# One load for the constants, the first query chunk ahead of the modulation chunks, and its products woven between the modulation pairs

## The chip, the cores and the metric

The kernel runs on one core of one Trainium2 chip. The time is the device time of one execution in microseconds (us); smaller is better. TensorE is PE in the profile (PEld its weight loads), VectorE is DVE, ScalarE is ACT, GpSimd is POOL and SyncE is SP.

## The reference

One layer of a diffusion backbone over 640 tokens (128 of context, 512 of latent) with 1024 channels, in float32. Cut to the part that the change touches:

```python
mod = silu(c) @ w_mod + b_mod                 # 6 x 1024 values, for context and latent each
shift1, scale1, gate1, shift2, scale2, gate2 = split(mod, 6)
h = rmsnorm(x, g_norm1) * (1 + scale1) + shift1
proj = h @ w_in + b_in                        # q, k, v, o, 32 gate columns, pooling, branch gates
y_a, C, n, m = mlstm_branch(q, k, v, o, gates, ...)      # two scans over time, eight heads
y_b = pool_branch(u_pool, ...)
x = x + gate1 * ((sigmoid(g_a) * (y_a @ w_a) + sigmoid(g_b) * (y_b @ w_b)) @ w_out)
x = x + gate2 * hier_moe(rmsnorm(x, g_norm2) * (1 + scale2) + shift2)   # 16 experts
```

No column of `proj` can be finished before all 1024 channels of `h` are there, and `h` needs the first third of `mod` (shift1 and scale1).

## The kernel before

Channels lie on the partitions. `xT`, `hn`, `hhi` and `hlo` each have eight blocks k of 128 channels x 640 tokens. Float32 products are made of three passes: each factor is split into a part `hi` that TensorE takes in its fast float32 form and a rest `lo`, and `three` adds hi*hi, hi*lo and lo*hi. ScalarE makes the hi part by a copy (`split_hi`, L573), VectorE the lo part by a subtraction (`split_lo`, L912).

Weights come in chunks of 1 MB (128 x 2048), in the order of one list (`wst`), through four buffers `raw[0]` to `raw[3]`. SyncE issues them in order (L373) and waits before each until its buffer is free: chunk c needs that chunk c-4 has been used. A chunk of the projection is free after its `split_lo`, a chunk of `w_mod` after the matmuls that read it. The list begins with the eight chunks of `w_mod` for shift1 and scale1, then come eight groups of one query or key chunk and two chunks of the rest of `w_mod`, then four value chunks.

The program up to the value stage:

- ScalarE issues eight loads of constants (L588: `cin`, `cst`, `col`, `wgr`, `bg`, `m0`, `wr`, `br`), all on one semaphore, and waits for all of them. SyncE issues the four loads of `xT`, then the chunks.
- Norm: ScalarE squares the eight blocks of `xT` (L594), GpSimd adds them (L435), TensorE sums over the partitions with a matrix of ones, ScalarE makes `rstd` (L580 and L581), VectorE multiplies (L935).
- First third of `mod`, in four rounds i: TensorE multiplies `csil` by two chunks (`mod_half`, L1489; two of them are a pair here), ScalarE copies the row out of PSUM (L601), TensorE turns it into columns (`mod_columns`), VectorE adds the bias and makes `gain` (L949, L952), then scales and shifts blocks 2i and 2i+1 of `hn` (L957); ScalarE makes `hhi` (L606) and VectorE `hlo` (L942). Round i+1 of TensorE starts behind round i.
- When all four rounds are through, TensorE takes the first query chunk block by block (L1521 on): for each k the 32 gate columns and the chunk's two blocks of 128 columns, 18 matmuls of 320 tokens, each time behind `hlo` of that k. The gates then go through ScalarE and VectorE (L609 to L971).
- j = 1 to 7: `block_q(j, 0)`, `mod_columns` of the group before, `mod_half`, `block_q(j, 1)`, `mod_half` (L1551 on). The `mod_half` calls of j = 0 stand right behind the first query chunk. Then the value stage (L1600 on), four chunks by five token tiles.

## Time and profile before

| what | value |
|---|---|
| median of three runs | 1082.78 us (1082.72 to 1090.57) |
| the profiled execution | 1087.06 us, span 1084.8 us |
| PE busy | 969.8 us (89%) |
| DVE, ACT, POOL busy | 599.0, 486.2, 139.2 us |
| mean granted TensorE clock | 0.951 |
| moved by DMA | 216.36 MB, 199 GB/s over the span |

The span is the time from the first to the last instruction of the profiled execution; its own time is the span and 2.3 us around it. In the page's 40 slices (27.1 us each) PE is at 0, 5, 8 and 8 tenths in the first four and at 9 in nearly all that follow; slice 30 has 2 and 8 around it, and the last two have 6 and 0.

### The profile page before, as it was taken

What the parts mean: (1) busy time and instruction counts of PE and PEld (TensorE: products, weight loads), DVE (VectorE), ACT (ScalarE), POOL (GpSimd) and SP (SyncE); (2) the same over time, 40 slices, a digit from 0 to 9 for tenths busy, and PEclk for the clock granted to TensorE, in tenths of its full rate; (3) what the DMA queues carried; (4) which work ended last, traced back from release to release, by engine and by line L of the source; (5) the groups of instructions that cost most, each with busy time, mean ns of one, the idle gap of its engine ahead of it and who ended that gap; (6) DMA issues with size and microseconds to landing.
All of it is one profiled execution on the core that took longest, in us unless ns stands there. A gap on an engine that the chain in (4) does not pass through costs nothing.

```text
span 1084.8 us, 13868 instructions
## 1 busy us (share of the span) xinstructions
PE 969.8 (89%) x5654; PEld 853.8 (79%) x5654; DVE 599.0 (55%) x751; ACT 486.2 (45%) x640; POOL 139.2 (13%) x135
## 2 busy tenths in 40 slices
PE   0588999999999999999999999982899999999960
PEld 0266888888788989999998998882788888888850
DVE  0432330123476758222115445536599999999986
ACT  2213222223557575222224123223578787888853
POOL 1200000000101000796000000001012111111120
PEclk9868999999999999999999999985899999999995
DMA  7453454551324223232221124522899999999945
GB/s 285 169 199 117 161 206 182 191 184 39 88 83 126 81 66 123 111 131 84 79 78 45 73 78 167 242 85 71 350 379 406 423 420 421 411 420 416 391 190 208
DMA packets 36063, 216.36 MB, mean 199 GB/s; under 512 B 4352, under 2 KB 4800, under 8 KB 15520
## 3 DMA queue, kind: packets, MB, share of 16 engines
q1 hardware_dynamic: 26064, 179.32, 42.4%
q0 software_dynamic: 8112, 32.53, 8.6%
q10 hardware_dynamic: 1824, 3.64, 0.9%
q8 instruction: 44, 0.72, 0.3%
q14 instruction: 19, 0.16, 0.1%
HBM read 200.68 MB, written 14.79 MB: 199 GB/s over the span
## 4 chain that ended last, share of the span: by engine, by line
PE 86%; DVE 6%; DMA 3%; ACT 3%; issue 1%; POOL 1%; ACTq 0%; DVEq 0%; POOLq 0%
PE ps L1449 81%; PE ps L1489 2%; DMA br<-in_br 1%; PE ps L1829 1%; POOL hn L435 1%; DMA yscr<-yb,slot_rows 1%; PE ps L1847 1%; DVE xr L1427 1%; DVE rowB L1424 1%; DVE hn L935 1%; DMA xg<-h2scr,slot_rows 1%; DVE xr L1431 0%; PE ps L1780 0%; PE ps L1712 0%; DVE OFF L1075 0%
## 5 line engine op out<-in xcount | busy, mean ns | idle before, releaser
L1449 PE MATMUL ps<-hhi,whi 128*128 128x320 f32 x672 | 156.7, 315 | 5.1 <-DVE wlo L917 5.1
L917 DVE TENSOR_TENSOR wlo<-raw,whi 128x2048 fp32r<-128x2048 f32 x29 | 68.0, 2348 | 167.8 <-ACT whi L576 167.8
L1449 PE MATMUL ps<-hlo,whi 128*128 128x320 f32 x672 | 154.5, 311 | 0.0
L1449 PE MATMUL ps<-hhi,wlo 128*128 128x320 f32 x672 | 154.5, 311 | 0.0
L1449 PEld LDWEIGHTS ps<-hhi,whi 128*128 128x128 f32 x672 | 113.1, 190 | 17.2 <-DVE wlo L917 6.0
L1449 PEld LDWEIGHTS ps<-hhi,wlo 128*128 128x128 f32 x672 | 113.7, 190 | 0.0
L1449 PEld LDWEIGHTS ps<-hlo,whi 128*128 128x128 f32 x672 | 113.5, 190 | 0.0
L576 ACT ACTIVATE whi<-raw 128x2048 fp32r<-128x2048 f32 x29 | 55.3, 1909 | 96.8 <-PE ps L1449 68.6
L1324 DVE TENSOR_TENSOR wlo<-raw,whi 128x2048 fp32r<-128x2048 f32 x32 | 72.6, 2288 | 5.2 <-ACT whi L844 5.2
L1324 DVE TENSOR_TENSOR olo<-raw,ohi 128x2048 fp32r<-128x2048 f32 x32 | 72.4, 2286 | 4.5 <-ACT ohi L844 4.5
L844 ACT ACTIVATE whi<-raw 128x2048 fp32r<-128x2048 f32 x32 | 61.3, 1919 | 18.3 <-PE ps L1449 18.3
L844 ACT ACTIVATE ohi<-raw 128x2048 fp32r<-128x2048 f32 x32 | 61.3, 1919 | 17.8 <-PE ps L1449 17.8
L534 POOL DMA_INDIRECT xg<-h2scr,slot_rows x16 | 18.6, 1160 | 360.3 <-DVE slot_rows L1377 246.5
L1449 PE MATMUL ps<-hhi,owh 128*128 128x320 f32 x160 | 58.2, 380 | 0.0
L1449 PE MATMUL ps<-whi,xgh 128*128 128x512 f32 x128 | 51.3, 401 | 2.4 <-DVE xgl L1331 2.4
L771 ACT ACTIVATE TH<-ps,col 128x640 f32<-128x640 f32 x16 | 12.7, 796 | 88.6 <-PE ps L1449 88.6
L1449 PE MATMUL ps<-ohi,xgh 128*128 128x512 f32 x128 | 50.6, 396 | 0.0
L1449 PE MATMUL ps<-whi,xgl 128*128 128x512 f32 x128 | 50.5, 394 | 0.0
L1449 PE MATMUL ps<-wlo,xgh 128*128 128x512 f32 x128 | 50.4, 393 | 0.0
L1449 PE MATMUL ps<-ohi,xgl 128*128 128x512 f32 x128 | 50.0, 391 | 0.0
L1449 PE MATMUL ps<-olo,xgh 128*128 128x512 f32 x128 | 49.9, 390 | 0.0
L544 POOL DMA_INDIRECT yscr<-yb,slot_rows x16 | 31.3, 1953 | 138.1 <-ACT yb L864 130.4
(314 smaller groups left out, 2095.9 us busy)
## 6 DMA issues: line engine op xcount, KB each, us to landing
raw<-in_wexp SPq DMA_DIRECT2D x64, 1024.0 KB, 9.0
raw<-in_wst SPq DMA_DIRECT2D x60, 1024.0 KB, 4.9
eraw<-in_wexp SPq DMA_DIRECT2D x32, 1024.0 KB, 8.3
nm<-negscr POOLq DMA_DIRECT2D x8, 640.0 KB, 7.1
wib<-wiscr POOLq DMA_DIRECT2D x8, 512.0 KB, 6.2
xT<-in_x SPq DMA_DIRECT2D x4, 640.0 KB, 7.1
xr<-in_xt SPq DMA_DIRECT2D x1, 2560.0 KB, 9.1
h2scr<-ht ACTq DMA_DIRECT2D x5, 512.0 KB, 3.6
```

Source lines behind the costliest of these rows:

```text
L435: gp.tensor_tensor(sq[:, 0, :], sq[:, 0, :], sq[:, k, :], ALU.add)\
L534: gp.indirect_dma_start(xg[p % 2][:, :], None, h2scr, bass.IndirectOffsetOnAxis(ap=slot_rows[:, 0, e:e + 1], axis=0)).then_inc(d_xg[p % 2] ...
L544: gp.indirect_dma_start(yscr, bass.IndirectOffsetOnAxis(ap=slot_rows[:, 1, e:e + 1], axis=0), yb[p % 2][:, :], None).then_inc(d_sc, 16)
L576: act.activation(dst[:, :], raw[raw_slot(c)][:, :], ACT.Copy).then_inc(hi_ready, 1)
L771: act.activation(halves(TH[:, gate_at(f), :]), pair(E_TH[f]), ACT.Tanh, scale=0.5, bias=col[:, 36 + f:37 + f]).then_inc(pair_free[E_TH[f] ...
L844: act.activation(ehi[i % ESPL][:, :], eraw[s][:, :], ACT.Copy).then_inc(e_hi, 1)
L917: dve.tensor_tensor(lo[:, :], raw[s][:, :], f32(hi[:, :]), ALU.subtract)\
L935: st.on(dve.tensor_tensor(hn[:, k, :], xT[:, k, :], rstd[:, :], ALU.mult))
L1324: dve.tensor_tensor(elo[i % ESPL][:, :], eraw[s][:, :], f32(ehi[i % ESPL][:, :]), ALU.subtract).then_inc(e_free[s], 1)
L1424: dve.scalar_tensor_tensor(rowB[:, t, :], rowB[:, t, :], wab[:, 1, t:t + 1], gate2[:, c, :], ALU.mult, ALU.mult).then_inc(f_y, 1)
L1449: return nc.tensor.matmul(out, lhsT, rhs, start=start, stop=stop)
L1489: last = nc.tensor.matmul(ps[32 * kk:32 * kk + 32, bank, :], csil[:, 4 * kh + kk, :], raw[slot][:, kk * 512:(kk + 1) * 512], start=kh == 0 ...
```

## The change

The constants become one tensor `small` (128 x 1440) with one load on SyncE's queue, ahead of `xT`; `wgr` has a load of its own behind `xT`. The first query chunk is the first of the list, ahead of the eight chunks of `w_mod`; the last group of `w_mod` stands right ahead of the values. VectorE adds the squares in place of GpSimd. ScalarE scales and shifts the blocks in place of VectorE (L609 of the new program). TensorE weaves the eight block steps of the first query chunk (`keys_outer`) between the pairs, and each group of the rest of `w_mod` is taken one j later, the last one in the value stage. The diff, cut to its core:

```diff
-AT_QK = N_MOD1
-AT_V = AT_QK + N_QK + N_MOD2
+AT_M1, AT_QK = 1, N_MOD1 + 1
+AT_V = N_MOD1 + N_QK + N_MOD2
...
+
+
+def m2_at(g):
+    return AT_QK + 1 + 3 * g if g < N_QK - 1 else AT_V - 2
...
 
         @block.sync
         def _(sp):
+            sp.dma_start(small[:, :], small_d).then_inc(d_const, 16)
             for k in range(0, KT, 2):
                 sp.dma_start(xT[:, k:k + 2, :], x_d[:, k:k + 2, :]).then_inc(d_x[k // 2], 16)
+            sp.dma_start(wgr[:, :, :], wg_d).then_inc(d_wg, 16)
             for s in range(NRAW):
                 sp.sem_inc(raw_free[s], 1)
...
             gp.memset(gOne[:, :], 1.0).then_inc(s_init, 1)
 
-            def sum_squares(sq, done, n=KT):
-
-                gp.wait_ge(done[0], 1)
-                for k in range(1, n):
-                    gp.wait_ge(done[0], k + 1)
-                    if k > 1:
-                        gp.wait_ge(done[1], k - 1)
-                    gp.tensor_tensor(sq[:, 0, :], sq[:, 0, :], sq[:, k, :], ALU.add)\
-                      .then_inc(done[1], 1)
-
-            sum_squares(hn, (s_sq, s_sum1))
...
-            smalls = [(cin[:, :, :], c_d), (cst[:, :], cst_d), (col[:, :], col_d),
-                      (wgr[:, :, :], wg_d), (bg[:, :], bg_d), (m0[:, :], m0_d),
-                      (wr[:, :, :], wr_d), (br[:, :], br_d)]
-            assert len(smalls) == N_SMALL
-            for dst, src in smalls:
-                act.dma_start(dst, src).then_inc(d_const, 16)
-            act.wait_ge(d_const, 16 * N_SMALL)
+            act.wait_ge(d_const, 16)
             act.activation(csil[:, :, 0:2], cin[:, :, :], ACT.Tanh, scale=0.5).then_inc(s_csil, 1)
             for k in range(KT):
                 if k % 2 == 0:
                     act.wait_ge(d_x[k // 2], 16)
                 act.activation(hn[:, k, :], xT[:, k, :], ACT.Square).then_inc(s_sq, 1)
+            act.wait_ge(d_wg, 16)
             act.activation(wgh[:, :, :], wgr[:, :, :], ACT.Copy).then_inc(s_wgh, 1)
             act.preload_act_table_set(LN_EXP)
+            split_hi(0, QH[0])
             act.wait_ge(s_ssq, 1)
             inv_rms(halves(rstd[:, :]), ps[:, 0:2, 0:HALF], D, s_rstd)
             for i in range(4):
-                chunk_used(act, 2 * i + 1)
-                act.activation(mrow1[:, i, :], ps[:, 2 + i, :], ACT.Copy).then_inc(s_mrow, 1)
-                if i == 3:
-                    split_hi(AT_QK, QH[0])
+                chunk_used(act, AT_M1 + 2 * i + 1)
+                if i >= 2:
+                    act.wait_ge(s_modT, i - 1)
+                act.activation(mrow1[:, i % 2, :], ps[:, 4, :], ACT.Copy).then_inc(s_mrow, 1)
+                act.wait_ge(s_gain, i + 1)
                 for k in (2 * i, 2 * i + 1):
-                    act.wait_ge(s_hn, k + 1)
+                    for c, a, b in ((0, 0, TC), (1, TC, T)):
+                        act.activation(hn[:, k, a:b], hn[:, k, a:b], ACT.Identity,
+                                       bias=mod[:, k, c:c + 1], scale=gain[:, k, c:c + 1])\
+                           .then_inc(s_hn, 1)
+                    act.wait_ge(s_hn, 2 * k + 2)
                     act.activation(hhi[:, k, :], hn[:, k, :], ACT.Copy).then_inc(s_hhi, 1)
+            split_hi(qk_at(1), QH[1])
 
             act.wait_ge(s_gps, 1)
...
-            for j in range(N_QK):
-                if j:
-                    act.wait_ge(q_used, j)
-                split_hi(AT_QK + 3 * j + 3, QH[(j + 1) % 2])
+            block_qk(0)
+            block_qk(1)
+            for j in range(1, N_QK):
+                act.wait_ge(q_used, j)
+                split_hi(qk_at(j + 1) if j < N_QK - 1 else AT_V, QH[(j + 1) % 2])
                 block_qk(2 * j)
                 block_qk(2 * j + 1)
-                mod_row2(j)
+                mod_row2(j - 1)
 
             act.wait_ge(q_used, N_QK)
             split_hi(AT_V + 1, QH[1])
+            mod_row2(N_QK - 1)
...
-                st.on(dve.tensor_tensor(hn[:, k, :], xT[:, k, :], rstd[:, :], ALU.mult))
+            for k in range(1, KT):
+                dve.wait_ge(s_sq, k + 1)
+                if k > 1:
+                    dve.wait_ge(s_sum1, k - 1)
+                dve.tensor_tensor(hn[:, 0, :], hn[:, 0, :], hn[:, k, :], ALU.add).then_inc(s_sum1, 1)
             dve.wait_ge(s_wgh, 1)
             dve.tensor_tensor(wgl[:, :, :], wgr[:, :, :], f32(wgh[:, :, :]), ALU.subtract)\
                .then_inc(s_wgl, 1)
+            split_lo(0, QH[0], QL[0])
+
+            def normalise(k):
+                st.on(dve.tensor_tensor(hn[:, k, :], xT[:, k, :], rstd[:, :], ALU.mult))
 
             def input_lo(k):
                 dve.wait_ge(s_hhi, k + 1)
                 dve.tensor_tensor(hlo[:, k, :], hn[:, k, :], f32(hhi[:, k, :]), ALU.subtract)\
                    .then_inc(s_hlo, 1)
 
+            dve.wait_ge(s_rstd, 1)
+            for k in range(4):
+                normalise(k)
             for i in range(4):
                 dve.wait_ge(s_modT, i + 1)
                 both = mod[:, 0:16, :].rearrange("p (s k) c -> p s k c", s=2)[:, :, 2 * i:2 * i + 2, :]
                 bias = col[:, B_MOD:B_MOD + 16].rearrange("p (s k) -> p s k", s=2)
-                st.do(dve.tensor_tensor(both, ps[:, 0, 448 + 8 * i:456 + 8 * i].rearrange(
+                st.do(dve.tensor_tensor(both, ps[:, 5, 0:8].rearrange(
                     "p (s k c) -> p s k c", s=2, c=2), by(bias[:, :, 2 * i:2 * i + 2].unsqueeze(3),
                                                           [P, 2, 2, 2]), ALU.add))
-                st.do(dve.scalar_tensor_tensor(
+                dve.scalar_tensor_tensor(
                     gain[:, 2 * i:2 * i + 2, :], mod[:, 8 + 2 * i:10 + 2 * i, :], 1.0,
-                    by(col[:, G_1 + 2 * i:G_1 + 2 * i + 2].unsqueeze(2), [P, 2, 2]), ALU.add, ALU.mult))
-                for k in (2 * i, 2 * i + 1):
-                    for c, a, b in ((0, 0, TC), (1, TC, T)):
-                        ins = dve.tensor_scalar(hn[:, k, a:b], hn[:, k, a:b], gain[:, k, c:c + 1],
-                                                mod[:, k, c:c + 1], ALU.mult, ALU.add)
-                    ins.then_inc(s_hn, 1)
-                if i == 3:
-                    split_lo(AT_QK, QH[0], QL[0])
+                    by(col[:, G_1 + 2 * i:G_1 + 2 * i + 2].unsqueeze(2), [P, 2, 2]), ALU.add, ALU.mult)\
+                   .then_inc(s_gain, 1)
+                if i < 2:
+                    normalise(4 + 2 * i)
+                    normalise(5 + 2 * i)
                 for k in (2 * i, 2 * i + 1):
                     input_lo(k)
+            split_lo(qk_at(1), QH[1], QL[1])
 
             dve.wait_ge(s_gate, 2)
...
+            def mod_pair(i):
+                if i:
+                    pe.wait_ge(s_mrow, i)
+                mod_half(AT_M1 + 2 * i, 0, 4)
+                mod_half(AT_M1 + 2 * i + 1, 1, 4)
+
+            def mod_turned(i):
+                if i:
+                    pe.wait_ge(s_gain, i)
+                pe.wait_ge(s_mrow, i + 1)
+                mod_columns(mrow1[:, i % 2, :], ps[:, 5, 0:8])
+
+            pe.wait_ge(d_const, 16)
+            square_sums(hn, s_sum1, s_ssq)
+            pe.wait_ge(s_csil, 3)
+            mod_pair(0)
+            mod_turned(0)
+            mod_pair(1)
+            pe.wait_ge(s_wgl, 1)
+            pe.wait_ge(s_rstd, 1)
+            chunk_split(0)
+            keys_outer(0)
+            mod_turned(1)
+            keys_outer(1)
+            mod_pair(2)
+            keys_outer(2)
+            mod_turned(2)
+            keys_outer(3)
+            mod_pair(3)
+            keys_outer(4)
+            mod_turned(3)
+            for k in (5, 6, 7):
+                keys_outer(k)
...
-            for j in range(N_QK):
-                if j:
-                    block_q(j, 0)
-                    pe.wait_ge(m_done, j - 1)
-                    pe.wait_ge(s_mrow, 4 + j)
-                    mod_columns(mrow, ps[:, 7, 0:8])
+            def mod2_turned(g):
+                pe.wait_ge(m_done, g)
+                pe.wait_ge(s_mrow, 5 + g)
+                mod_columns(mrow, ps[:, 7, 0:8])
+
+            for j in range(1, N_QK):
+                block_q(j, 0)
+                if j >= 2:
+                    mod2_turned(j - 2)
                 else:
                     pe.wait_ge(s_gate, 2)
-                mod_half(AT_QK + 3 * j + 1, 0, 6)
-                if j:
-                    block_q(j, 1)
+                mod_half(m2_at(j - 1), 0, 6)
+                block_q(j, 1)
                 pe.sem_inc(q_used, 1)
-                mod_half(AT_QK + 3 * j + 2, 1, 6)
+                mod_half(m2_at(j - 1) + 1, 1, 6)
...
                 for t in range(NT):
                     value_block(c, t)
                     if c == 0 and t == 0:
-                        pe.wait_ge(m_done, N_QK - 1)
-                        pe.wait_ge(s_mrow, 4 + N_QK)
-                        mod_columns(mrow, ps[:, 7, 0:8])
-                    if c == 0 and t == 3:
+                        mod2_turned(N_QK - 2)
+                        mod_half(m2_at(N_QK - 1), 0, 6)
+                        mod_half(m2_at(N_QK - 1) + 1, 1, 6)
+                    if c == 0 and t == 2:
+                        mod2_turned(N_QK - 1)
+                    if c == 0 and t == 4:
```

Three places in the programs. In the rows `raw_67` to `raw_70` are the four weight buffers of the program before and `raw_61` to `raw_64` those of the new one; `whi_71` and `whi_65` are the hi part of the first query chunk; `mrow` is a row of `mod`, and a matmul from it is a `mod_columns`. L1449 and L1489 before are L1466 and L1506 now.

TensorE at its start, before:

```order
L1449 MATMUL ps<-hn,cst 128x320 [waits s_sum1,s_csil,d_const]
...
L1489 MATMUL ps<-raw_67,csil 32x512 [waits raw_full0]
...
L1489 MATMUL ps<-raw_68,csil 32x512 [waits raw_full1]
...
L1449 MATMUL ps<-cst,mrow_83 128x2 [waits s_mrow,s_rstd]
...
L1489 MATMUL ps<-raw_69,csil 32x512 [waits raw_full2]
```

and now:

```order
L1466 MATMUL ps<-hn,small 128x320 [waits s_sum1,d_const]
...
L1506 MATMUL ps<-raw_62,csil 32x512 [waits raw_full1,s_csil]
...
L1506 MATMUL ps<-raw_63,csil 32x512 [waits raw_full2]
...
L1466 MATMUL ps<-small,mrow_77 128x2 [waits s_mrow]
...
L1506 MATMUL ps<-raw_64,csil 32x512 [waits raw_full3,s_mrow]
...
L1506 MATMUL ps<-raw_61,csil 32x512 [waits raw_full0]
...
L1466 MATMUL ps<-hhi,wgh 48x320 [waits raw_free0,s_hlo,s_rstd,s_wgl]
```

The first block step now stands behind the second pair; the second pair's last chunk uses the buffer of the first query chunk.

ScalarE in the first round, before and then now:

```order
L596 ACT_TABLE_LOAD
L580 ACTIVATE rstd<-ps,cst 128x640 [waits s_ssq]
L581 ACTIVATE rstd<-rstd 128x640 [waits act_steps]
L601 ACTIVATE mrow_83<-ps 128x512 [waits raw_free1]
L606 ACTIVATE hhi<-hn 128x640 [waits s_hn] x2
```

```order
L582 ACTIVATE whi_65<-raw_61 128x2048 [waits raw_full0]
L586 ACTIVATE rstd<-ps,small 128x640 [waits s_ssq]
L587 ACTIVATE rstd<-rstd 128x640 [waits act_steps]
L605 ACTIVATE mrow_77<-ps 128x512 [waits raw_free2]
L609 ACTIVATE hn<-hn,mod,gain 128x128 [waits s_gain]
L609 ACTIVATE hn<-hn,mod,gain 128x512
L613 ACTIVATE hhi<-hn 128x640 [waits s_hn]
```

The hi part of the first query chunk is made ahead of `rstd`, and two operations per block have come to ScalarE.

TensorE from the last chunk of the query stage into the value stage, before and then now (L1601 and L1643 turn the gathered values of `mod`):

```order
L1489 MATMUL ps<-raw_70,csil 32x512 [waits raw_full3]
...
L1449 MATMUL ps<-whi_71,hhi 128x512 [waits v_free,q_free,raw_free0]
...
L1449 MATMUL ps<-cst,mrow 128x2 [waits s_mrow,m_done]
...
L1449 MATMUL ps<-whi_71,hhi 128x512 [waits v_free,q_free]
...
L1601 MATMUL ps<-cst,mst 64x128 [waits s_mst]
```

```order
L1506 MATMUL ps<-raw_62,csil 32x512 [waits raw_full1]
...
L1466 MATMUL ps<-whi_65,hhi 128x512 [waits v_free,q_free,raw_free0]
...
L1466 MATMUL ps<-small,mrow 128x2 [waits s_mrow,m_done]
...
L1506 MATMUL ps<-raw_63,csil 32x512 [waits raw_full2]
...
L1506 MATMUL ps<-raw_64,csil 32x512 [waits raw_full3]
...
L1466 MATMUL ps<-small,mrow 128x2 [waits s_mrow,m_done]
...
L1643 MATMUL ps<-small,mst 64x128 [waits s_mst]
```

Two chunks of `w_mod` and a second turning have come into the first value chunk.

## Rows read from the trace of the kernel before

**Rows 1.** Busy time by window: window, length, engines, granted clock, DMA share, GB/s.

```profile
0.00:97.00 97.00, 47.20 (x261) 32.13 (x262) 27.23 (x52) 26.51 (x35) 11.66 (x13) 0.87 0.54 202
102.00:560.00 458.00, 456.27 (x3007) 416.28 (x3007) 186.21 (x383) 166.80 (x358) 76.78 (x89) 1.00 0.34 117
```

**Rows 2.** The chain of waits, 0 to 110 us: start, length, what.

```profile
4.81 16.04 DMA br<-in_br
...
22.49 1.54 POOL hn L435
...
34.22 2.49 PE ps L1449 x4
...
38.33 5.97 DVE hn L935 x8
...
53.40 0.61 ACT mrow L601
54.05 1.87 PE ps L1449 x8
...
66.33 21.75 PE ps L1449 x132
...
92.57 1.81 ACT whi L576
...
96.82 10.39 PE ps L1449 x56
```

**Rows 3.** DMA 0 to 22 us in 40 slices, total; landing of `xT`, of `raw`.

```profile
GB/s 0 0 0 112 168 214 410 382 425 424 413 401 449 430 390 429 409 417 404 448 404 380 473 410 358 462 415 381 421 428 384 445 391 376 453 420 403 417 283 30
DMA packets 2112, 7.73 MB, mean 351 GB/s; under 512 B 576, under 2 KB 960, under 8 KB 1600
DMA to landing us min/median/max: 4.4/7.1/9.6
DMA to landing us min/median/max: 4.8/6.7/17.4
```

**Rows 4.** Two modulation pairs in the timeline, then windows as in group 1.

```profile
36.62 3.64 PE L1489 MATMUL ps<-raw,csil 128*32 128x512 f32 x16
42.03 1.92 PE L1489 MATMUL ps<-raw,csil 128*32 128x512 f32 x16
...
44.00:47.90 3.90, 0.00 (x0) 0.00 (x0) 3.74 (x10) 1.94 (x3) 0.00 (x0) 0.93 0.99 376
48.00:62.00 14.00, 12.57 (x56) 6.42 (x56) 7.05 (x17) 5.89 (x7) 0.00 (x0) 0.50 0.88 327
66.30:70.80 4.50, 4.47 (x17) 4.15 (x18) 1.40 (x2) 0.00 (x0) 0.00 (x0) 0.50 0.69 240
71.10:88.00 16.90, 16.90 (x116) 15.87 (x115) 0.00 (x0) 0.00 (x0) 0.00 (x0) 1.00 0.00 1
```

**Rows 5.** Groups by form on ACT and DVE: busy us, mean ns, idle before.

```profile
L594 ACT ACTIVATE hn<-xT 128x640 f32<-128x640 f32 x8 | 5.1, 719 | 0.0
L672 ACT ACTIVATE DG<-nmd,a_tok 128x128 f32<-128x128 f32 x80 | 25.1, 398 | 11.1 <-PE ps L1449 9.8 <-DVE nmd L1054 1.3
L681 ACT ACTIVATE OFF<-nm,a_tok 128x384 f32<-128x384 f32 x16 | 9.9, 616 | 0.0
L942 DVE TENSOR_TENSOR hlo<-hn,hhi 128x640 fp32r<-128x640 f32 x8 | 6.2, 820 | 0.3
L917 DVE TENSOR_TENSOR wlo<-raw,whi 128x2048 fp32r<-128x2048 f32 x2 | 4.6, 2287 | 1.1 <-ACT whi L576 1.1
```

**Rows 6.** One j of the query stage: chain of waits, then ACT's timeline.

```profile
107.21 0.99 PE ps L1489 x8
108.21 7.24 PE ps L1449 x48
...
116.44 8.02 PE ps L1449 x56
...
121.48 1.91 ACT L576 ACTIVATE whi<-raw 128x2048 fp32r<-128x2048 f32 x1 [4.37 <-DMA raw<-in_wst]
```

More of the change, by code:

```diff
@@ L80 @@
 B_IN, B_MOD, G_1, G_2, G_F, G_N, P_S, W_END = 0, 52, 100, 108, 116, 124, 132, 136
+S_COL = 1088
+S_C = S_COL + W_END
+S_BG, S_M0, S_WR, S_BR = S_C + 16, S_C + 24, S_C + 32, S_C + 32 + KT * (EG + NE)
+S_END = S_BR + 24
 class Steps:
@@ L145, in sem @@
             return ctx.enter_context(nc.semaphore(name))
-        cst = at("cst", 0, [P, C_END])
+        small = at("small", 0, [P, S_END])
+        cst, col = small[:, 0:C_END], small[:, S_COL:S_COL + W_END]
+        cin = small[:, S_C:S_C + 2 * KT].rearrange("p (k c) -> p k c", c=2)
+        bg, m0 = small[0:GP, S_BG:S_BG + 1], small[0:R16, S_M0:S_M0 + 1]
+        wr = small[:, S_WR:S_BR].rearrange("p (k e) -> p k e", k=KT)
+        br = small[:, S_BR:S_BR + EG + NE]
         ident, ones = cst[:, C_ID:C_ID + P], cst[:, C_ONE:C_ONE + P]
@@ L151, in layer_kernel @@
         eps = cst[:, C_EPS:C_EPS + 1]
-        col = at("col", 4.25, [P, W_END])
-        mod = at("mod", 4.875, [P, 48, 2])
-        gain = at("gain", 5.25, [P, KT, 2])
-        cin = at("cin", 5.3125, [P, KT, 2])
-        half_gn = at("half_gn", 5.6875, [P, KT])
-        a_tok = at("a_tok", 5.75, [P, NT, R16])
+        mod = at("mod", 5.625, [P, 48, 2])
+        gain = at("gain", 6, [P, KT, 2])
+        half_gn = at("half_gn", 7.5625, [P, KT])
+        a_tok = at("a_tok", 7.25, [P, NT, R16])
         em_tok = at("em_tok", 6.375, [P, NT, R16])
@@ L932, in _ @@
             st.on(dve.tensor_scalar(half_gn[:, :], col[:, G_N:G_N + KT], 0.5, None, ALU.mult))
-            dve.wait_ge(s_rstd, 1)
-            for k in range(KT):
-                st.on(dve.tensor_tensor(hn[:, k, :], xT[:, k, :], rstd[:, :], ALU.mult))
+            for k in range(1, KT):
[3 more added lines that the diff above has]
+                dve.tensor_tensor(hn[:, 0, :], hn[:, 0, :], hn[:, k, :], ALU.add).then_inc(s_sum1, 1)
             dve.wait_ge(s_wgh, 1)
@@ L1506, in square_sums, with keys_outer @@
                 last.then_inc(done, 1)
-            pe.wait_ge(d_const, 16 * N_SMALL)
-            pe.wait_ge(s_csil, 3)
-            square_sums(hn, s_sum1, s_ssq)
-            for i in range(4):
-                mod_half(2 * i, 0, 2 + i)
-                mod_half(2 * i + 1, 1, 2 + i)
-                if i == 0:
-                    pe.wait_ge(s_rstd, 1)
-                pe.wait_ge(s_mrow, i + 1)
-                mod_columns(mrow1[:, i, :], ps[:, 0, 448 + 8 * i:456 + 8 * i])
-            pe.wait_ge(s_wgl, 1)
-            chunk_split(AT_QK)
-            for k in range(KT):
+            def keys_outer(k):
                 pe.wait_ge(s_hlo, k + 1)
@@ L1535, in _ @@
                         last.then_inc(q_ready, 1)
+            def mod_pair(i):
[29 more added lines that the diff above has]
+                keys_outer(k)
+            pe.sem_inc(q_used, 1)
             pe.sem_inc(blk_ready, E_U)
             def block_q(j, b):
-                chunk = AT_QK + 3 * j
+                chunk = qk_at(j)
                 e = 2 * j + b
```

51 lines of the change are left out of this document (28 added, 23 removed).

## The prediction

> **What bounds the kernel now.** I read the busy time by window first. From 102 to 560 us TensorE works 456.3 of 458 us at the full clock; in the first 97 us it works 47.2 [rows 1]. So the time that a reordering of the first stage wins arrives at the end only as far as `block_q(1, 0)`, which starts at 96.82, starts earlier: nothing behind it has a gap to soak it up, and nothing behind it is touched up to the value stage but for the places named below.
>
> The chain of waits then says what fills these 97 us [rows 2]. The last of eight loads on ScalarE's queue, `br`, lands 16.04 us after its issue, at 20.85, and nothing has begun until then. GpSimd adds seven squares at 1.54 each (11.6 us with their handoffs), TensorE's ones take 2.49 and VectorE's eight products 5.97. Then come rounds of a row copy (0.61), a turning (1.87) and a pair (3.6), one behind the other, until TensorE gets to the first query chunk at 66.33 for 21.75 us. Behind it TensorE waits while the gates go through ScalarE and VectorE, since the next query chunk is split behind them in both queues (ACT 92.57); it resumes at 96.82, and its first block takes 10.39 us where 8.02 is usual [rows 2, 6].
>
> That last figure is the clock. A pair takes 3.64 us in one place and 1.92 in another [rows 4]. After 3.9 us without a matmul the granted clock goes to 0.50 (1.2 GHz) and stays there through 48 to 62 us, where TensorE is busy 12.57 of 14 us with pairs and turnings; it rises only after some 4.5 us of the first query chunk. At 0.50 a matmul of that chunk takes 4.47/17 = 0.263 us, at the full 2.4 GHz 16.90/116 = 0.146, so a step of 18 matmuls takes 4.73 or 2.62.
>
> **Step 1, loads.** 7.73 MB move in the first 22 us, at some 415 GB/s once they run [rows 3], and all have landed at 20.9 [rows 2]. So what stands B MB deep in the queue lands at about 20.9 - (7.73 - B)/0.415. The change moves the same bytes, in the order constants 0.74 MB, `xT` 2.62, `wgr` 0.20, chunks 1.05 each. By this the constants land at 4.1 (I take 5, as the shortest `xT` load took 4.4 [rows 3]), the last of `xT` at 10.4, chunks 0 to 3 at 13.4, 15.9, 18.4 and 21.0. Chunk 4 needs buffer 0, which is free at 18, and follows at 23.5.
>
> **Step 2, norm.** The last two squares end at 11.8, VectorE's sum at 12.7 (0.82 per add, the price of `hlo` [rows 5], beside the squares, in place of 1.54 on GpSimd), the ones at 15.2. ScalarE splits chunk 0 by 15.5, so `rstd` is there at 17.1 (two operations of 0.8), VectorE's lo part (2.29 [rows 5]) at 17.9, and four products of 0.75 at 20.9.
>
> **Step 3, the first pair.** It waits for chunk 2: 18.4, half a pair at the slow rate 1.8, row copy 0.6, turning 1.9, `gain` 0.4: 23.2. So the norm is hidden here, by 2 us; the constants, the adds and the products have left the path.
>
> **Step 4, ScalarE's new work.** The trace has no scale-and-shift of `hn` on ScalarE. Its nearest rows are `DG` (128 columns with a bias from memory, 25.1/80 = 0.31 a piece) and `OFF` (384 columns, 0.62, against 0.40 for 128: 0.085 per 100 columns, so 0.73 for 512) [rows 5]. I take 1.05 for both parts of a block, then 0.72 for `hhi` and small handoffs: 1.8 per block. The lower end is 1.5, were they to overlap as the eight squares do (5.1 for eight of 719 ns), the upper 2.2. The Trainium skill, ScalarE: Activation LUTs, on the chain from input to output, gives 93 ns for each operand that is a pointer; these have two, so by it a block takes 2.0. VectorE's copy of this work goes (L957), and so costs nothing: `hlo` at 0.82 is all that is left there per block.
>
> **Step 5, steps and pairs woven.** The second pair runs from 22.8 to 26.5 slow. `hlo` of block 0 is ready at 23.2 + 1.8 + 0.8 = 25.8, so the first step starts at 26.5. The clock is the question. I let it rise at 28, some 5 us after the second pair began, as at 66.3 [rows 4]; the first step then ends at 29.8. Behind it TensorE has seven steps (18.3), two pairs (3.8) and three turnings (0.8 each, the difference of 8.02 and 7.24 [rows 6]): 24.5, hence 54.3. Each step's `hlo` is there in time but that of block 6 (0.4 to wait after the last turning). The next query chunk is split by ScalarE and VectorE behind block 7: 50.5 + 1.9 + 2.4 = 54.8, level with TensorE. With 0.05 to 0.1 for each of some 15 handoffs I put the start of `block_q(1, 0)` at **56.0**, against 96.82: 40.8 won. The gates (8.7 us on the path before) now lie beside `block_q(1, 0)`; `mod_half` needs them only 7 us after its start, and they take 1.6 up to there.
>
> **Step 6, what comes behind.** The first block runs warm: -2.4. Two `mod_half`, which stood in the old wait, are now in TensorE's full stretch: +2.0. The value stage gets one turning, j = 1 has lost one: 0. The first value chunk needs the buffer that the first `mod_half` of j = 7 gives back, no longer the second one of j = 6. From such a release to the hi part's start it took 121.48 - 116.44 = 5.0 us, then 1.91 and 2.29 and handoffs: 9.4; TensorE gets there in 7.24 + 0.99 = 8.2 [rows 5, 6]. That is a new wait of +1.2. Behind it the stores of the scan rows leave ScalarE some 7 us later; their readers work after the third value chunk, over 25 us on. Together +0.8.
>
> **The sum.** 40.8 - 0.8 = 40.0 us. The profiled execution took 1087.06 us, its span 1084.8; by the sum they become 1047.1 and 1044.8. The median of the three runs is 4.3 below that execution, and I set the sum against it: 1082.8 - 40.0 = **1042.8 us**.
>
> **Rivals.**
> - *The clock rises late.* For it speaks that pairs and turnings alone did not lift it in 14 us [rows 4], and they are woven in here; against it that each step is dense. If only step and pair 2 together lift it, at about 38, 4.5 us more: 1047, up to 1053 with a second fall. If it stays at 0.50 for the whole weave, TensorE's start comes to 78.5 and the first block is slow as well: 18.3 - 0.8 - 2.4 = 15.1 won, 1068.
> - *The constants land late.* One queue is no promise of order: `br` landed 16 us after its issue. If `small` is complete only with the last of `xT`, at 11.4, squares to `rstd` end at 22.1, chunk 4 is issued at 22.8, and the first step starts 3.4 us later: 1046. The Trainium skill, DMA: Bandwidth & Descriptors, on HWDGE ordering, says that completion is not first in, first out per issuing engine. By that rule this case would be open for every load here.
> - *It does not arrive.* The value chunk's wait, or a load that comes late once all that uses it is 40 us earlier, gives the gain back: within 1% of now. Against it: 117 GB/s on average in 102 to 560 us [rows 1].
> - *Slower.* TensorE stays at 1.2 GHz beyond the weave, through the query blocks: each j of 17.2 us then takes 13.7 more (96 matmuls at +0.114, two halves at +0.85, a turning). From the second such j on the whole is slower than before; through all seven it is 1068 + 7 x 13.7 = 1164. It decides at `block_q(1, 0)`. Against it: 96.82 us, where one such block from the cold needed 2.4 us more and not 5.5 [rows 2, 6].
>
> **How the numbers follow.** Forecast as summed, 1039 to 1047: 0.68. Constants late 0.08; clock late 0.14; slow through the weave 0.05; not arriving 0.03; slower 0.02. The range 1037 to 1053 takes the first three, with the ends of step 4 (0.3 less or 0.4 more per block, two blocks of it on the path) and the 2.4 us that a warm start or no wait in step 6 would give below. A change of 1% is 10.8 us, about what a measurement of this kernel can tell from none. All cases but the last two lie beyond it: faster 0.95, within 1% 0.03, slower 0.02.
>
> **What would show it.** In the trace after: ScalarE's first operation at 5 us and not 20.9; no GpSimd adds; the first pair's second half at 18.4; the first step near 26.5; a step of 2.6 us from the second on (4.7 means the clock); `block_q(1, 0)` at 54 to 58; 1.2 us of idle ahead of the first value chunk. I am wrong if the first step starts after 31, if the steps stay at 4.7 us beyond the third, or if new gaps over 1 us stand behind the value stage.

## The result and the profile after

The changed kernel takes **1045.52 us** (median of 4 runs, 1044.59 to 1046.88), the kernel before 1082.95 beside it (4 runs, 1082.72 to 1090.57): ratio 0.964, 95% interval 0.960 to 0.968. The profiled execution took 1046.88 us with a span of 1045.1. The forecast was 1042.8 in a range of 1037 to 1053.

Busy time and clock by window, as in [rows 1]:

```profile
0.00:57.00 57.00, 39.04 (x257) 28.47 (x258) 26.75 (x42) 33.37 (x47) 0.93 (x6) 0.97 0.80 314
57.00:520.00 463.00, 459.92 (x3032) 417.91 (x3031) 188.97 (x384) 171.31 (x364) 76.50 (x89) 1.00 0.36 122
```

The stretch in which TensorE has no gaps starts some 40 us earlier. The first stage holds 39.0 us of TensorE's work in place of 47.2, and GpSimd works 0.93 us in it in place of 11.66. The chain of waits of the changed kernel (start, length, what), against [rows 2]:

```profile
2.85 8.32 DMA xT<-in_x
...
11.19 1.36 ACT hn L594 x2
...
12.98 1.28 ACT L597
...
14.27 1.92 ACT whi L582
...
16.22 2.30 DVE wlo L927
...
18.54 5.60 DMA raw<-in_wst
...
24.18 1.93 PE ps L1506 x8
26.11 6.93 PE ps L1466 x44
...
46.94 1.21 ACT hn L609 x2
...
49.82 12.53 PE ps L1466 x84
62.34 1.00 PE ps L1506 x8
```

The last `xT` load replaces `br` as the first thing waited for. Then comes chunk 4 (the row at 18.54: issued when buffer 0 is free, landed at 24.14), and from there TensorE's own work sets the time, but for one block's `gain` to `hlo` ahead of 49.82, for which TensorE waits 0.65 us. The row at 62.34 is the first `mod_half` of the later chunks; `block_q(1, 0)` lies 48 matmuls (7.2 us) ahead of it, from 55.1. Before, the half behind the same block stands at 107.21.

The load of constants in the list of DMA issues (KB, us from issue to landing):

```profile
small<-in_small SPq DMA_DIRECT2D x1, 720.0 KB, 4.1
```

The new work on ScalarE and the split behind it, by form, 0 to 60 us, as in [rows 5]:

```profile
L609 ACT ACTIVATE hn<-hn,mod,gain 128x512 f32<-128x512 f32 x8 | 6.4, 800 | 0.0
L613 ACT ACTIVATE hhi<-hn 128x640 fp32r<-128x640 f32 x8 | 5.9, 738 | 0.3
L609 ACT ACTIVATE hn<-hn,mod,gain 128x128 f32<-128x128 f32 x8 | 3.9, 487 | 12.2 <-DVE gain L971 12.2
```

The clock, as in [rows 4]. First the two halves of the first pair in the timeline:

```profile
16.78 1.35 PE L1506 MATMUL ps<-raw,csil 128*32 128x512 f32 x8
19.16 1.07 PE L1506 MATMUL ps<-raw,csil 128*32 128x512 f32 x8 [1.03 <-DMA raw<-in_wst]
```

Then windows around the first step (granted clock third from the end):

```profile
24.00:25.00 1.00, 0.82 (x4) 0.20 (x8) 0.56 (x1) 1.00 (x3) 0.00 (x0) 0.62 0.98 410
...
27.00:28.00 1.00, 1.00 (x7) 0.87 (x6) 0.12 (x1) 0.00 (x0) 0.00 (x0) 0.68 1.04 434
28.00:29.00 1.00, 1.00 (x9) 1.00 (x9) 0.00 (x0) 0.00 (x0) 0.00 (x0) 1.00 1.03 426
```

The first pair ran in 1.35 and 1.07 where a half at the low clock takes 1.8. The row has the clock low (0.50, the 1.2 GHz level) only from about 24.2 to 27.6 (the shares of 0.62 and 0.68). Ahead of that it is no guide: it reads 1.00 from the first microsecond on, also where the first pair of the kernel before takes 3.64 us (36.62, [rows 4]). There the times of the matmuls tell the speed. Last, the end of the query stage, against [rows 6]:

```profile
165.82 1.04 PE ps L1506 x8
...
166.87 4.91 DMA raw<-in_wst
...
171.86 1.92 ACT whi L582
...
173.81 2.30 DVE wlo L927
...
176.16 3.80 PE ps L1466 x20
```

Each earlier stretch is followed by the next half at once; here a block stands between 166.86 and 176.16, and the matmuls of the value chunk wait for `wlo`. The list of waits gives 1.1 us of idle on TensorE for it. It is the one new wait between the first stage and the value stage.

How far the two profiled executions are apart: at that half 44.9 us (107.21 and 62.34), behind the gates' first work in the value stage 40.8 (238.33 and 197.54), at the experts' prologue 40.2 (574.98 and 534.77), at the last expert's down projection 39.7 (1031.60 and 991.86), in the span 39.7, in the time 40.2. Where the 1.1 us between the value stage and the end of the span go was not followed up.

### The profile page after: what moved, and what is told of

It reads as the page before. It is cut to its first block, busy times and chain, and to the rows that moved or that the text cites. A ratio compares the mean times of both kernels' runs of the same rounds, so it can differ in the third digit from the quotient of the medians.

```text
span 1045.1 us, 13870 instructions
## 1 busy us (share of the span) xinstructions
PE 960.8 (92%) x5654; PEld 846.5 (81%) x5654; DVE 599.7 (57%) x742; ACT 495.6 (47%) x656; POOL 127.2 (12%) x128
## 4 chain that ended last, share of the span: by engine, by line
PE 81%; issue 7%; DVE 5%; DMA 4%; ACT 2%; POOL 1%; SPq 0%; DVEq 0%; POOLq 0%; ACTq 0%
PE ps L1466 76%; PE ps L1506 2%; PE ps L1871 1%; DMA raw<-in_wst 1%; DMA xT<-in_x 1%; DMA nm<-negscr 1%; DMA yscr<-yb,slot_rows 1%; PE ps L1889 1%; DVE xr L1444 1%; DVE rowB L1441 1%; DMA xg<-h2scr,slot_rows 1%; DVE xr L1448 0%; DVE wlo L927 0%; PE ps L1822 0%; PE ps L1754 0%
## 5 line engine op out<-in xcount | busy, mean ns | idle before, releaser
L1466 PE MATMUL ps<-hhi,whi 128*128 128x320 f32 x672 | 155.1, 312 | 0.0
L1466 PE MATMUL ps<-hlo,whi 128*128 128x320 f32 x672 | 153.1, 309 | 0.0
L1466 PE MATMUL ps<-hhi,wlo 128*128 128x320 f32 x672 | 153.1, 309 | 0.0
L1466 PEld LDWEIGHTS ps<-hhi,whi 128*128 128x128 f32 x672 | 111.7, 188 | 11.1 <-issue 5.9
L1466 PEld LDWEIGHTS ps<-hhi,wlo 128*128 128x128 f32 x672 | 112.4, 188 | 0.0
L1466 PEld LDWEIGHTS ps<-hlo,whi 128*128 128x128 f32 x672 | 112.3, 188 | 0.0
L854 ACT ACTIVATE whi<-raw 128x2048 fp32r<-128x2048 f32 x32 | 61.3, 1919 | 18.5 <-PE ps L1466 18.5
L540 POOL DMA_INDIRECT xg<-h2scr,slot_rows x16 | 18.5, 1155 | 360.8 <-DVE slot_rows L1394 246.5
L1466 PE MATMUL ps<-hhi,owh 128*128 128x320 f32 x160 | 58.2, 380 | 0.0
L781 ACT ACTIVATE TH<-ps,small 128x640 f32<-128x640 f32 x16 | 12.7, 796 | 88.6 <-PE ps L1466 88.6
L1466 PE MATMUL ps<-whi,xgh 128*128 128x512 f32 x128 | 51.5, 402 | 2.4 <-DVE xgl L1348 2.4
L1466 PE MATMUL ps<-ohi,xgh 128*128 128x512 f32 x128 | 50.7, 396 | 0.0
L1466 PE MATMUL ps<-whi,xgl 128*128 128x512 f32 x128 | 50.5, 394 | 0.0
L1466 PE MATMUL ps<-wlo,xgh 128*128 128x512 f32 x128 | 50.4, 394 | 0.0
L1466 PE MATMUL ps<-ohi,xgl 128*128 128x512 f32 x128 | 50.0, 391 | 0.0
L1466 PE MATMUL ps<-olo,xgh 128*128 128x512 f32 x128 | 49.8, 389 | 0.0
```

The source lines that it names most:

```text
L540: gp.indirect_dma_start(xg[p % 2][:, :], None, h2scr, bass.IndirectOffsetOnAxis(ap=slot_rows[:, 0, e:e + 1], axis=0)).then_inc(d_xg[p % 2] ...
L781: act.activation(halves(TH[:, gate_at(f), :]), pair(E_TH[f]), ACT.Tanh, scale=0.5, bias=col[:, 36 + f:37 + f]).then_inc(pair_free[E_TH[f] ...
L854: act.activation(ehi[i % ESPL][:, :], eraw[s][:, :], ACT.Copy).then_inc(e_hi, 1)
L1466: return nc.tensor.matmul(out, lhsT, rhs, start=start, stop=stop)
```

## Experiments

All runs stand beside the kernel before on the same chip; the ratio is to it. Positions (`block_q(1, 0)` and so on) are from each run's own trace.

### The changed kernel again, and the kernel before again

No edit. It gives the scatter against which small effects have to stand.

> The changed kernel once more, as the base for the three others of this call: 1045.5 us, within 1.5. Theory: its first 97 us hold no clock state that changes from run to run, since TensorE is nearly always busy from 24 us on; its runs then lie within 2 us of each other. Rival: the start is as unsettled as in the kernel before (1082.7 to 1090.6), and single runs lie 4 us and more above the lowest.

Measured: 1044.87 us (1043.47 to 1045.44), ratio 0.964 (0.962 to 0.967). The runs lie within 2 us, but not for the reason given: the start does hold a clock state that changes. In this trace the second half of the second pair took 1.06 us in place of 1.93, and the clock didn't fall. Chunk 4 landed at 25.05, 0.9 later than in the first trace. A third time, beside other kernels:

> The changed kernel, unchanged, as the base of this call: 1044 to 1046.5 us, block_q(1,0) at 54.5 to 55.5, the wait ahead of the first value chunk 1.1 us. Nothing is disputed in it.

Measured: 1045.42 (1044.02 to 1047.00), ratio 0.966 (0.963 to 0.969). The kernel before, for a second trace:

> The kernel before, for a second trace. Its runs lie between 1077.9 and 1090.6 us, 12.7 apart, those of the changed kernel within 3.5. Theory: most of that spread comes from the start, where chunk by chunk TensorE waits for bare pairs and the clock rises or does not, so that between 0 and 97 us a faster or slower run differs from the first trace, while each stage from block_q(1,0) on takes the same to 0.5 us. Rival: the spread comes from later stages (experts, 540 us on), which both kernels have, and then the stages behind 97 us differ by 1 us or more between the two traces of the kernel before.

Measured: 1078.58 us, span 1076.8, 8.0 below its first trace. Its chain of waits:

```profile
53.98 1.07 PE ps L1449 x8
...
63.60 20.87 PE ps L1449 x132
...
93.22 9.91 PE ps L1449 x56
...
1047.67 3.39 DMA yscr<-yb,slot_rows
```

In the first trace the turning took 1.87, the first query chunk 21.75 from 66.33, and `block_q(1, 0)` started at 96.82 and took 10.39 [rows 2]. Here the clock rose between the rounds, and it starts 3.6 earlier; by the value stage it is 4.1 (234.25 against 238.33). So half of the 8.0 us is what the theory said. The other half it had not: the last store of expert results, 3.39 us here, 7.47 in the first trace. Both the theory and its rival hold for a half each, in this one pair of traces. In the traces of the changed kernel that store took 7.26, 7.02 and 7.31.

### Constants in eight loads (undoes the load)

```diff
-            sp.dma_start(small[:, :], small_d).then_inc(d_const, 16)
-            sp.dma_start(wgr[:, :, :], wg_d).then_inc(d_wg, 16)
...
+            for a, b, n in ((S_C, S_C + 16, P), (0, C_END, P), (S_COL, S_COL + W_END, P), (None, None, P),
+                            (S_BG, S_BG + 8, GP), (S_M0, S_M0 + 8, R16), (S_WR, S_BR, P),
+                            (S_BR, S_BR + EG + NE, P)):
+                if a is None:
+                    act.dma_start(wgr[:, :, :], wg_d).then_inc(d_const, 16)
+                else:
+                    act.dma_start(small[0:n, a:b], small_d[0:n, a:b]).then_inc(d_const, 16)
-            act.wait_ge(d_const, 16)
+            act.wait_ge(d_const, 128)
...
```

> The changed kernel with the constants in eight loads on ScalarE's queue again, and all engines waiting for all of them. Theory: they land at 20.9 as before; squares end at 26, rstd at 31, the chunk split at 32 and with it chunk 4 at 37, so the first step starts some 13 us later: 1058.5 us. Rival: the chunks of weights set the start anyway (chunk 2 lands at 18.4 and chunk 4 at 24), and the late constants cost only the difference of 4 us: 1049.5.

Measured: 1057.87 (1054.25 to 1058.69), ratio 0.975 (0.972 to 0.979). Its chain of waits:

```profile
4.75 16.18 DMA small<-in_small
...
62.95 12.52 PE ps L1470 x84
```

The piece that landed last, in its list of DMA issues:

```profile
small<-in_small ACTq DMA_DIRECT2D x1, 10.0 KB, 16.2
```

10 KB took 16.2 us. They landed in turn by time of issue, between two chunks of SyncE's queue: chunk 2, issued at 4.43, landed at 19.6, this piece (4.75) at 20.9, chunk 3 (4.94) at 22.1. Of the 7.73 MB that moved in the first 22 us 6.82 were SyncE's. The first step starts at 39.92, 13.8 us later than in the changed kernel. The clock didn't fall here (a first stretch of 6.25 us against 6.93), so that 13.1 are left at the point that stands at 49.82 there and at 62.95 here.

### The kernel before with the one load alone

The eight loads on ScalarE's queue become one on SyncE's ahead of `xT`; all else is as before.

```diff
+            sp.dma_start(small[:, :], small_d).then_inc(d_const, 16)
             for k in range(0, KT, 2):
                 sp.dma_start(xT[:, k:k + 2, :], x_d[:, k:k + 2, :]).then_inc(d_x[k // 2], 16)
+            sp.dma_start(wgr[:, :, :], wg_d).then_inc(d_wg, 16)
...
-            for dst, src in smalls:
-                act.dma_start(dst, src).then_inc(d_const, 16)
```

> The kernel before with only the one load of constants on SyncE's queue ahead of xT (wgr behind it), nothing else changed. Theory: GpSimd's adds begin at 7.9 in place of 22.5 and all rounds follow, 14.6 us earlier: 1068 us. Rival: the rounds wait for the chunks of weights, which land at up to 20.9 either way, and only 4 us are won: 1079.

Measured: 1069.71 (1068.48 to 1072.56), ratio 0.987 (0.984 to 0.990): 13.4 us below the kernel before. The first query chunk in its chain:

```profile
51.83 21.82 PE ps L1452 x132
```

14.5 us earlier than 66.33 [rows 2]. By the ratios, medians and traces of these two kernels the load is worth 11 to 14.5 us, about a third of the whole.

### Squares added on GpSimd (undoes VectorE's adds)

```diff
...
-                dve.tensor_tensor(hn[:, 0, :], hn[:, 0, :], hn[:, k, :], ALU.add).then_inc(s_sum1, 1)
...
+                gp.tensor_tensor(hn[:, 0, :], hn[:, 0, :], hn[:, k, :], ALU.add).then_inc(s_sum1, 1)
```

> The seven adds of squares go back to GpSimd, all else as in the changed kernel. Theory: 7 x 1.65 from 7.9 end at 19.4 in place of 14.2, the ones delay the first pair behind them on TensorE, and the first step starts near 30.5 and not at 26.1: 4.4 us more, 1050. Rival: the adds lie beside the loads of the chunks (chunk 4 lands at 24.2): no change within 1 us.

Measured: 1049.21 (1047.86 to 1051.45), ratio 0.968 (0.965 to 0.971), 3 to 4 us above the changed kernel. Its chain:

```profile
18.17 3.40 POOL hn L448
...
32.93 6.25 PE ps L1466 x44
...
55.96 12.53 PE ps L1466 x84
```

The last add takes 3.40 us where the others take 1.54. In the timeline VectorE's lo split of the first chunk lies across it:

```profile
16.51 3.67 DVE L932 TENSOR_TENSOR wlo<-raw,whi 128x2048 fp32r<-128x2048 f32 x1 [1.55 <-ACT whi L587]
```

The split took 2.29 in the changed kernel. From 16.50 to 21.57 stand two adds and one split, 5.1 us where their times alone add up to 5.4: nearly as if the two engines had worked in turn. The theory, which had both rates unchanged, put the end of the adds at 19.4 and the first step at 30.5; they came at 21.57 and 32.93. That is 6.8 us later than the changed kernel's 26.11, and 6.1 are left at 55.96 (against 49.82), as the clock didn't fall here. The medians show less, and the forecast of 1050 was met with a wrong term.

### Steps and pairs not woven (undoes the weave)

```diff
             mod_turned(0)
-            mod_pair(1)
+            for i in (1, 2, 3):
+                mod_pair(i)
+                mod_turned(i)
...
-            keys_outer(0)
-            mod_turned(1)
-            ...
+            for k in range(KT):
+                keys_outer(k)
```

> TensorE takes all four pairs and turnings first and the eight block steps behind them; everything else as in the changed kernel. Theory (the weave hides the chain turning, gain, two blocks on ScalarE, row copy, turning): that chain runs bare three times at some 5.7 us, the steps begin at 40 and block_q(1, 0) at 63 to 65 in place of 55: 8 to 10 us more, 1054 us. Rival: TensorE's own work is the bound and its order is worth little: 2 us more at most.

Measured: 1057.00 (1056.24 to 1057.33), ratio 0.976 (0.973 to 0.979). Its chain:

```profile
27.43 1.85 PE ps L1466 x8
...
40.08 32.35 PE ps L1466 x200
```

The rounds of copy, turning and wait stand bare up to 40.08, then all steps run without a gap. `block_q(1, 0)` starts at 65.2, 10.1 us later than in the changed kernel; the ratios (0.976 against 0.964 to 0.966) say 11 to 13. Some of this is the clock: a turning and a pair ran slow here (1.84 and 3.64 us where 1.05 and 1.92 are usual), 2.5 us, against 1.6 that the slow stretch cost in the changed kernel.

### Scale and shift on VectorE

```diff
-                        act.activation(hn[:, k, a:b], hn[:, k, a:b], ACT.Identity,
-                                       bias=mod[:, k, c:c + 1], scale=gain[:, k, c:c + 1])\
-                           .then_inc(s_hn, 1)
...
+                st.wait()
+                dve.wait_ge(s_gain, i + 1)
...
+                        dve.tensor_scalar(hn[:, k, a:b], hn[:, k, a:b], gain[:, k, c:c + 1],
+                                          mod[:, k, c:c + 1], ALU.mult, ALU.add).then_inc(s_hn, 1)
```

> The scale-and-shift of the blocks goes back from ScalarE to VectorE, all else as in the changed kernel. Theory: TensorE is the bound of the weave, so the place of this work matters only at the last turning, where ScalarE's 1.2 us per block make TensorE wait 0.7 us for block 6; VectorE takes 0.8 per block, so 0 to 0.9 us less. Rival: VectorE is crowded by products, lo parts and the next chunk's split, and the first step starts later: 1 to 3 us more.

Measured: 1046.66 (1044.55 to 1048.37), ratio 0.966 (0.964 to 0.969). Its chain:

```profile
23.43 1.51 DVE hn L974 x4
24.95 1.47 DVE hn L949 x2
26.42 0.75 DVE hlo L953
...
27.30 7.93 PE ps L1467 x44
```

The four pieces cost VectorE 1.51 us, but the next products stand behind them in its queue and ahead of `hlo`: from `gain` to the `hlo` of block 0 it takes 3.8 us here and 2.9 in the changed kernel. That 1.0 us is the edit's. The first step is at 27.3 in place of 26.1, and its stretch took 7.93 us in place of 6.93, as the clock stayed at 0.50 until 31.0; that part can't be put down to the edit. The median is 1.8 us above that of the repeated changed kernel, and the intervals overlap, so a loss is likely but not shown.

### First value chunk loaded one place earlier

Chunk order: the value chunk 0 goes ahead of the last group's second modulation chunk, in the load table and in both split queues.

```diff
-def m2_at(g):
-    return AT_QK + 1 + 3 * g if g < N_QK - 1 else AT_V - 2
+def m2_at(g, half=0):
+    if g < N_QK - 1:
+        return AT_QK + 1 + 3 * g + half
+    return AT_V - 2 + 2 * half
+
+
+def v_at(c):
+    return AT_V + c if c else AT_V - 1
```

> The first value chunk changes places in the list of chunks with the last one of the modulation, so its buffer is the one that split_lo of the last key chunk frees, a whole j earlier. Theory (the new wait of step 6 is set by the buffer): the 1.1 us of idle ahead of the first value chunk go, 1.0 to 1.2 us less than the changed kernel. Rival: the wait is ScalarE's or VectorE's queue (the hi part stands behind q_used), then the idle stays and the time is the same within 0.2.

Measured: 1041.50 (1038.92 to 1043.77), ratio 0.961 (0.958 to 0.964). Once more:

> The early value chunk once more, beside the changed kernel on the same chip. The wait that it removes is 1.1 us in the trace; the medians of its first run said 3.4 below the changed kernel. Theory: 1.1 us is the effect and the other 2.3 were luck of five runs whose spread is 5 us: this time 0 to 2.5 below the changed kernel of this call. Rival: the early chunk also shortens something behind the value stage, and the difference is 3 us or more again; then a stretch between 200 and 990 us is shorter in its trace.

Measured: 1042.50 (1040.64 to 1044.55), ratio 0.963 (0.960 to 0.966). The end of its query stage:

```profile
166.96 7.24 PE ps L1474 x48
174.20 0.99 PE ps L1514 x8
175.20 3.74 PE ps L1474 x20
```

The wait is gone, and the value stage behind it comes 1.1 us earlier than in the changed kernel run beside it (196.51 against 197.63), with `block_q(1, 0)` level. The medians say 3.4 and 2.9. Of that 1.1 is shown. The spans of this second comparison differ by 1.9; the 0.8 more lies between 535 and 731 us, in one projection of 24 matmuls (7.57 against 8.34), which took 7.1 to 8.7 in the other traces, and was the slower one here in the first comparison (8.37 against 7.40). So the rest of the 3 us stays open; no trace ties it to this edit.

### Constants in two parts

On top of the last one. Only what the norm and the turnings need (0.18 MB) goes first; the other 0.55 MB follow behind chunk 3.

```diff
-            sp.dma_start(small[:, :], small_d).then_inc(d_const, 16)
+            sp.dma_start(small[:, P:2 * P], small_d[:, P:2 * P]).then_inc(d_const, 16)
+            sp.dma_start(small[:, C_MF:S_WR], small_d[:, C_MF:S_WR]).then_inc(d_const, 16)
...
+                if c == 3:
+                    for a, b in ((0, P), (2 * P, C_MF), (S_WR, S_END)):
+                        sp.dma_start(small[:, a:b], small_d[:, a:b]).then_inc(d_vb, 16)
```

> As the kernel with the exchanged value chunk, and 0.55 MB of the 0.74 MB of constants (identity, masks, iota, router weights) are loaded behind chunk 3. Theory: up to the second pair everything stands in the queue of the DMA engines, at 0.42 MB per us, so the fifth chunk and with it the first step come 1.3 us earlier, and all is 2.4 us below the changed kernel (1.1 of it from the exchange). Rival: chunk 4 waits for its buffer (freed at 18.5) and not for bandwidth, then only 1.1 in all.

Measured: 1045.12 (1043.45 to 1045.78), ratio 0.965 (0.962 to 0.967): nothing won over the changed kernel, and 3.6 us above the early value chunk alone. Its chain:

```profile
18.18 6.98 DMA raw<-in_wst
...
25.20 1.06 PE ps L1518 x8
26.27 7.77 PE ps L1478 x44
```

The row at 25.20 is the second half of the second pair. Chunk 4 lands at 25.16; in the three traces of the changed kernel it landed at 24.14, 24.32 and 25.05 (the last one beside this run). The landings give the reason why nothing was won: chunk 3 at 21.29, the three late pieces at 21.5 to 22.7, and chunk 4 one chunk's time (2.5 us) behind them. The same bytes as before stand ahead of chunk 4, where the theory had 0.55 MB less. So nothing could be won there, and chunk 4 came 0.1 to 1.0 us later. Another part is the clock: it was low from 26.5 to 29.9 under the first steps (a stretch of 7.77 us, where the early value chunk alone had 6.21). At the value stage this trace is 2.0 us behind that one (197.35 against 195.36), 0.9 of it from chunk 4 and 1.1 from the clock; the rest of the 3.6 stays open. The part of the loads was put to the test by moving them behind the second modulation chunk of group 0:

```diff
-                if c == 3:
+                if c == m2_at(0, 1):
```

> The early value chunk together with constants in two parts, the late 0.55 MB now issued where the value bias is, behind the modulation chunk of group 0, and no longer behind chunk 3. My theory of the e8_late_constants run is that its saving was taken back by the 0.55 MB standing ahead of chunk 4 in SyncE's queue (chunk 4 landed at 25.2 us there, 24.1 in the changed kernel). If so, chunk 4 lands at about 22.9 us here (0.55 MB at some 0.42 MB per us is 1.3 us less than 24.1), the first woven step starts at about 25, and block_q(1,0) 1.0 to 1.3 us earlier than in the changed kernel: 1.0 to 1.3 below the early value chunk alone, 2.1 to 2.4 below the changed kernel by the trace. Rival: the start is bound by the first norm's chain on VectorE and not by chunk 4, which then lands with nobody waiting: chunk 4 is early, but the first step stays within 0.4 us of 26.0. Second rival: the clock rises no earlier (it falls behind the first pairs for longer), and the steps run at 7.8 us each: no gain.

Measured: 1040.15 (1037.43 to 1042.61), ratio 0.961 (0.957 to 0.964), the **fastest** of all. Its second half of the second pair in the timeline:

```profile
23.56 1.06 PE L1518 MATMUL ps<-raw,csil 128*32 128x512 f32 x8 [1.14 <-DMA raw<-in_wst]
```

Its chain:

```profile
24.84 6.26 PE ps L1478 x44
...
47.87 12.53 PE ps L1478 x84
```

And the chain of the changed kernel run beside it:

```profile
24.37 1.94 PE ps L1506 x8
26.30 6.91 PE ps L1466 x44
...
49.99 12.51 PE ps L1466 x84
```

Chunk 4 is 0.8 earlier (it landed at 23.52; the theory said 1.2 earlier, at 22.9), and so is everything from `xT` on; the late part's place in the queue is what held chunk 4 back in the run before. The whole is 2.1 earlier at the last row of the two chains. The other 1.3 us come from the clock, which stayed at 1.00 in this trace (a half pair of 1.06, a first stretch of 6.26). One trace doesn't tell whether that comes with this order; the changed kernel has had it too (below).

## Why the prediction was right

**What bounds it.** Right: of 40.8 us that are won up to the value stage, 39.7 are there in the span. The gap near 700 us (PE at 4 and 5 tenths in the page's slices) soaked nothing up: it is itself on the chain of waits, a row of small VectorE operations ahead of the experts, and moved along.

**Step 1, loads.** Right, 0.6 to 0.8 us too early. Constants landed at 4.8 (5 taken), the last of `xT` at 11.2 (10.4), chunk 2 at 19.1 (18.4), chunk 4 at 24.1 (23.5). One row was misread: 20.9 is the landing of `br`, and not of all 7.73 MB; the fourth chunk took 17.4 us from its issue [rows 3] and landed at 22.3. Some 0.42 MB/us held for all; the rival of late constants did not come. The Trainium skill, DMA: Bandwidth & Descriptors, says on HWDGE ordering that completion is not first in, first out per issuing engine. No load of SyncE's queue in this trace overtook an earlier one. In the eight-load kernel, with two queues, one load did: chunk 0, issued at 3.56, landed at 14.41, 0.27 us ahead of a small piece issued on ScalarE's queue at 3.13.

**Step 2, norm.** Squares, adds, ones and products had the right prices (0.82 per add, 2.47, 0.76 per product), but `rstd` was there at 18.5 and not at 17.1. The step that was wrong is the adds. VectorE's and ScalarE's timelines:

```profile
7.82 6.41 DVE L947 TENSOR_TENSOR hn<-hn 128x640 f32<-128x640 f32 x7 [2.03 <-ACT hn L594]
16.89 0.79 ACT L586 ACTIVATE rstd<-ps,small 128x640 f32<-128x640 f32 x1 [0.70 <-PE ps L1466]
```

The seven adds were taken to keep up with the squares and to end 0.8 us behind them (12.7). Each waits for the one before, 0.93 us from start to start, so they were bound by themselves and ended at 14.2. A load of ScalarE's table (12.98, 1.28 us), which the program orders ahead of the split, was missing too. It delayed the split of the first chunk (`wlo` at 18.5 and not 17.9), but not `rstd`: ScalarE was free 0.70 us before the sums came. The first four products were done at 21.5. All this cost nothing, as the first block then waited for `gain` (22.4).

**Step 3, first pair.** Chunk 2 came at 19.1 (18.4 forecast), but the half pair took 1.07 and the turning 1.05, at the times of the fast clock, where 1.8 and 1.9 were summed: `gain` at 22.4, not 23.2.

**Step 4, scale and shift.** 1.20 for both parts and 0.74 for `hhi`: 1.94 per block, inside the bounds of 1.5 to 2.2, 0.14 above the 1.8 taken from rows. The estimate of 2.0 by the Trainium skill, ScalarE: Activation LUTs, was nearer (the figure of 93 ns stands there under What ACT_TABLE_LOAD costs). Both pieces' own means add up to 1.29 and they overlap by 0.09.

**Step 5, the weave.** The first step at 26.1 (26.5), the clock up at 27.6 (28), `block_q(1, 0)` at 55.1 (56.0). That the start came so close is in part luck. The forecast had the clock low all the way from the first pair; it was fast there and low only from 24.2, and what it saved in the first pair and turning made up for chunks 2 and 4, each 0.6 to 0.7 late. What held the first step was chunk 4 and then a slow half pair (1.93), and where the clock falls changes from execution to execution (below). Of the 0.9 us the first step has 0.4; the wait for block 6 was 0.65 where 0.4 was forecast; the rest would be handoffs below the 0.05 to 0.1 assumed. Undoing the weave costs 10 to 13 us, undoing VectorE's adds 3 to 6, undoing the one load 11 to 14.5. What is left of 37 to 39, some 4 to 15 us if the parts add up, would be the order that puts the first query chunk's steps ahead of the gates and later modulation chunks. Before, TensorE waits for the gates and the split behind them from 88.1 to 96.8 [rows 2], and now it has work there. That order was not tried alone, and so is argued and not shown.

**Step 6, what comes behind.** 41.7 us ahead at `block_q(1, 0)`, 40.8 in the value stage: 0.9 given back, 0.8 forecast. The new wait was 1.1 where 1.2 was forecast, by the path that was named (the buffer that the first `mod_half` gives back), and the early value chunk took it away.

**The sum** was 40.0; the two profiled executions differ by 40.2. What missed, by 2.7 us, is the base: the sum was set against the median of the runs before, which lay 4.3 below its profiled execution, while the profiled execution after lies 1.4 above its median. The second trace of the kernel before shows what those 4.3 could be: 3.6 to 4.1 us of slow clock in the rounds of the first stage, the very stage that was rewritten, and 4.1 in the last store. The first of these was in the 40.0 already; a run without it had less to win. In the three comparisons the medians differ by 37.4 to 38.7 us.

**Rivals.** Clock late: no, 27.6 (at the latest 31.0, in the kernel with scale and shift on VectorE). Not arriving: no. Slower by a low clock in the query blocks: no, 1.00 from 57 to 520 us.

## What to carry to other kernels

A forecast summed from one traced execution is a difference between two executions; before it is set against a median, ask which of its terms (here a slow clock in the rewritten stage) other runs don't have. Constants in small pieces on another queue waited behind the bulk that was issued before them, so they go in one load at the head of the bulk's own queue; but bytes that nobody needs yet must stand behind the last load that something waits for, not just behind the first few. Before a chain of dependent operations is taken as hidden beside another engine, multiply its own spacing by its length (here seven adds at 0.93 us). Before a small difference is put down to an edit, compare the clock of the two traces at that place. When an engine's work moves earlier, look for the buffer release that now comes last, and move that one load up.
